# The first layer's gate columns in three chunks of 512 and its last value columns in two of 384, with the fill beside the attention set from 64 to 48

## The reference

```
proj = h @ w_in
na_qkv, na_gate, dn_qkv, dn_gate, dn_ba, mem_q, mem_gate = split_cols(
    proj, [3 * NA_W, NA_W, 3 * DN_W, DN_W, 4 * DN_HEADS, MEM_W, MEM_W])
...
na_o = merge_heads(neighbourhood_attention(q, k, v, na_rpb)) * jax.nn.silu(na_gate)
dn_o = deltanet_branch(dn_qkv, dn_ba, ...) * jax.nn.silu(dn_gate)
mem_o = memory_branch(mem_q, mem_n, w_mem_kv, ...) * jax.nn.silu(mem_gate)
return x + jnp.concatenate([na_o, dn_o, mem_o], axis=-1) @ w_out
```

## Time and profile before

| what | value |
|---|---|
| median of 3 runs | 3140.31 us (3139.92 to 3143.08) |
| time of the profiled execution | 3142.65 us |
| its span, first to last instruction | 3140.9 us |
| mean granted TensorE clock | 0.990 |
| PE, DVE, ACT busy | 97%, 58%, 48% of the span |
| the attention of the first layer | from 554.4 to 662.0 us of the span |

### The profile page before, as it was taken

One profiled execution on the slowest core, in us unless ns is written; L12 is line 12 of the kernel. 1 busy time (PEld: TensorE's weight loads), 2 busy tenths in 40 slices (PEclk: granted clock), 3 DMA queues, 4 the chain that ended last, 5 costly groups with the idle time before them and its releaser, 6 DMA issues.

```text
span 3140.9 us, 36907 instructions
## 1 busy us (share of the span) xinstructions
PE 3049.4 (97%) x15084; PEld 2588.2 (82%) x15084; DVE 1810.5 (58%) x2348; ACT 1517.4 (48%) x2332; POOL 9.4 (0%) x10
## 2 busy tenths in 40 slices
PE   6999999999999999999999999999999999999999
PEld 5878888878877788989888888888889888888887
DVE  4686666555555455665666545555575675554554
ACT  4654333554555555544546444444554545444443
POOL 0000000000000000000000000000000000000000
PEclk8999999999999999999999999999999999999999
DMA  6553222456544556544544656656544544555654
GB/s 230 163 174 108 94 68 94 135 181 227 176 160 148 172 174 209 183 147 147 174 161 161 203 196 204 207 185 209 190 155 139 175 161 163 188 199 189 218 190 155
DMA packets 273433, 534.92 MB, mean 170 GB/s; under 512 B 8912, under 2 KB 50000, under 8 KB 271216
## 3 DMA queue, kind: packets, MB, share of 16 engines
q1 hardware_dynamic: 268976, 509.12, 49.3%
q10 hardware_dynamic: 4288, 23.44, 1.9%
HBM read 523.09 MB, written 9.44 MB: 170 GB/s over the span
## 4 chain that ended last, share of the span: by engine, by line
PE 85%; DVE 7%; ACT 5%; DVEq 2%; issue 1%; ACTq 0%; DMA 0%; SPq 0%
PE acc L377 25%; PE acc L379 25%; PE acc L378 25%; DVE w_lo L340 2%; PE tb L671 1%; ACT w_hi L330 1%; PE tb L875 1%; PE tb L2230 1%; PE tb L882 1%; PE tb L881 1%; PE tb L2105 1%; DVE stat L2058 0%; PE tb L2103 0%; DVE sq L2056 0%; PE tb L1132 0%
## 5 line engine op out<-in xcount | busy, mean ns | idle before, releaser
L340 DVE TENSOR_TENSOR w_lo<-raw,w_hi 128x1024 fp32r<-128x1024 f32 (+3 forms) x1008 | 1140.4, 1170 | 678.6 <-ACT w_hi L330 668.6
L330 ACT ACTIVATE w_hi<-raw 128x1024 fp32r<-128x1024 f32 (+3 forms) x1008 | 986.3, 1016 | 570.2 <-PE acc L379 548.1
L377 PE MATMUL acc<-w_hi,x_hi 128*128 128x512 f32 (+4 forms) x2880 | 1126.7, 391 | 29.9 <-DVE w_lo L340 29.8
L379 PE MATMUL acc<-w_hi,x_lo 128*128 128x512 f32 (+4 forms) x2880 | 1092.3, 379 | 0.0
L378 PE MATMUL acc<-w_lo,x_hi 128*128 128x512 f32 (+4 forms) x2880 | 1090.8, 379 | 0.0
L377 PEld LDWEIGHTS acc<-w_hi,x_hi 128*128 128x128 f32 x2880 | 547.1, 190 | 124.3 <-DVE w_lo L340 32.2
L379 PEld LDWEIGHTS acc<-w_hi,x_lo 128*128 128x128 f32 x2880 | 546.0, 190 | 93.9
L378 PEld LDWEIGHTS acc<-w_lo,x_hi 128*128 128x128 f32 x2880 | 547.5, 190 | 84.6
L377 PE MATMUL acc<-w_hi,mB_hi 128*128 128x512 f32 x256 | 100.6, 393 | 0.0
L379 PE MATMUL acc<-w_hi,mB_lo 128*128 128x512 f32 x256 | 99.8, 390 | 0.0
L378 PE MATMUL acc<-w_lo,mB_hi 128*128 128x512 f32 x256 | 99.7, 389 | 0.0
(11 more groups left out here) (483 smaller groups left out, 3473.1 us busy)
## 6 DMA issues: line engine op xcount, KB each, us to landing
raw<-in_h_w_in SPq DMA_DIRECT2D x184, 1024.0 KB, 4.9
raw<-in_o_w_in SPq DMA_DIRECT2D x56, 1024.0 KB, 5.0
raw<-in_e_w_in SPq DMA_DIRECT2D x48, 1024.0 KB, 5.0
raw<-in_h_w_branch SPq DMA_DIRECT2D x48, 1024.0 KB, 5.0
raw<-in_h_w_out SPq DMA_DIRECT2D x32, 1024.0 KB, 4.9
raw<-in_h_w_in SPq DMA_DIRECT2D x40, 768.0 KB, 4.3
raw<-in_e_w_out SPq DMA_DIRECT2D x16, 1024.0 KB, 5.0
raw<-in_o_w_out SPq DMA_DIRECT2D x16, 1024.0 KB, 5.0
```

Source lines behind the costliest of these rows:

```text
L330: act.activation(k.w_hi[:, a % HI_SLOTS, rows, :width], k.raw[:, a % SLOTS, rows, :width], ACT.Copy).then_inc(k.hi_ready, 1)
L340: e.tensor_tensor(k.w_lo[:, a % SLOTS, rows, :width], k.raw[:, a % SLOTS, rows, :width], k.w_hi[:, a % HI_SLOTS, rows, :width].bitcast(F32 ...
L377: pe.matmul(out, x_hi[:, tok], wh, start=first, stop=False)
L379: mm = pe.matmul(out, x_lo[:, tok], wh, start=False, stop=last)
```

## The change

The columns of the weight matrix are laid out on the host so that the DN gate and the NA gate stand next to each other (1536 columns), and are projected in three chunks of 512; the middle one is copied out in parts, two blocks to `dgate` and two to `ngate`. The last 768 columns of NA q, k, v become two chunks of 384 in place of one of 512 and one of 256. The gates' steps fall from 64 to 48, and `ATT_FILL` with them, so that the same eight steps, now 512 wide, stay for after the attention. The two silus on ACT move from after visit 26 to after visit 33, and DVE's multiplications from after visit 30 to after visit 36. (All lines of the changed file stand two lower from here on: L1151 is L1153 there.)

```diff
+DN_COL, GATE_COL, MEM_COL = 2304, 4632, 6168
...
-DN_FILL, ATT_FILL = 104, 64
+DN_FILL, ATT_FILL = 104, 48
...
-    c["N"] = add(k, w, 0, 4, x, into(k.na, 0), **a)
-    c["N"] += add(k, w, 2048, 1, x, into(k.na, 16, 2), width=256, **a)
-    c["MQ"] = add(k, w, BA_COL + BA, 1, x, into(k.mq4, 0), **a)
-    c["MG"] = add(k, w, BA_COL + BA + 512, 1, x, into(k.mg, 0), **a)
-    c["DG"] = add(k, w, 5376 + BA, 1, x, into(k.dgate, 0), **a)
-    c["DG"] += add(k, w, 5376 + BA + 512, 1, x, into(k.dgate, 4, 2), width=256, **a)
-    c["NG"] = add(k, w, 2304, 1, x, into(k.ngate, 0), **a)
-    c["NG"] += add(k, w, 2304 + 512, 1, x, into(k.ngate, 4, 2), width=256, **a)
+    c["N"] = add(k, w, 0, 3, x, into(k.na, 0), **a)
+    c["N"] += add(k, w, 1536, 2, x, into(k.na, 12, 3), width=384, **a)
+    c["MQ"] = add(k, w, MEM_COL, 1, x, into(k.mq4, 0), **a)
+    c["MG"] = add(k, w, MEM_COL + 512, 1, x, into(k.mg, 0), **a)
+    g = add(k, w, GATE_COL, 1, x, into(k.dgate, 0), **a)
+    g += add(k, w, GATE_COL + 512, 1, x, lambda i: lambda t: (k.dgate[:, 4:6, t, :], k.ngate[:, 0:2, t, :]), "parts", **a)
+    g += add(k, w, GATE_COL + 1024, 1, x, into(k.ngate, 2), **a)
+    c["DG"], c["NG"] = g[:2], g[1:]
...
-        if i == 26:
+        if i == 33:
             act_silu(k, act, PART_DN, k.named["DG"])
             act_silu(k, act, PART_MEM, k.named["MG"])
...
-        elif i == 30:
+        elif i == 36:
             dve.drain()
             dve_gated(k, dve, PART_DN, 1)
             dve_gated(k, dve, PART_MEM, 2)
...
-    return np.concatenate([w[:, :5376], w[:, BA_COL:BA_COL + BA], w[:, 5376:BA_COL], w[:, BA_COL + BA:]], axis=1)
+    na, nag, dn, dng, ba, mem = np.split(w, [2304, 3072, 5376, 6144, 6144 + BA], axis=1)
+    return np.concatenate([na, dn, ba, dng, nag, mem], axis=1)
```

More of the change, by code:

```diff
@@ L35 @@
 BA = 4 * DN_H
-BA_COL = 6144
+DN_COL, GATE_COL, MEM_COL = 2304, 4632, 6168
 O_Q, O_K, O_V, O_G = (0, 12, 24), (4, 16, 28), (8, 20, 32), (44, 48, 52)
@@ L504, in plan_even @@
     a = dict(by="act", rstd=2)
-    c["D"] = add(k, w, 3072, 4, x, into(k.dn_p, 0), need=lambda kt: kt // 2 + 1, **a)
-    c["D"] += add(k, w, 3072 + 2048, 1, x, lambda i: lambda t: (k.dn_p[:, 16:18, t, :], k.ba_cols[:, t, :]), "parts",
+    c["D"] = add(k, w, DN_COL, 4, x, into(k.dn_p, 0), need=lambda kt: kt // 2 + 1, **a)
+    c["D"] += add(k, w, DN_COL + 2048, 1, x, lambda i: lambda t: (k.dn_p[:, 16:18, t, :], k.ba_cols[:, t, :]), "parts",
                   width=256 + BA, **a)
```

## The result

The changed kernel takes 3147.53 us in the median of 15 runs (3144.85 to 3152.03), the kernel before on the same chips 3141.53 (3139.37 to 3143.69). The ratio is 1.0022, with a 95% interval of 1.0014 to 1.0030 (the ratio is taken over all runs; the two medians alone give 1.0019): slower by 6 us. That is clear of the interval, and close to the 0.2% that the prediction set as the limit of what can be told from no change. The profiled execution took 3147.54 us, its span is 3145.7, against 3142.65 and 3140.9 before.

A forecast was written before the change was run, and what follows sets the result against it. PE's issue time and waits bound the kernel (PE busy 97%). Matmuls -1.0, attention waits with low clock +5.1, deltanet -0.4 sum to +3.7 us: 3144.0 us from a median of 3140.31, range 3138 to 3149 (the forecast's own 3142 to 3146.3).

The forecast's parts named there:

- The matmuls: PE, deltanet steps 48 to 79: 192 matmuls of 384 columns replace 288 of 256, saving 1.0 us.
- The last pair: Attention, unit 8: PE waits 6.5 us for the exponential behind copies, silus and a quad's split.
- The fourth pair: Attention, units 6 and 7: the split of visit 27 between two exponentials makes PE wait 2.7 us.
- Elsewhere: Attention: waits of 1.4 us in the second pair, 0.7 in the third, none found in the first.
- The low clock: Attention: half clock costs 1.6 us after the wait of 6.5 and 0.8 after that of 2.7.
- The attention's sum: First fill to last product: about 106.5 us, with steps and visits 92.8 and waits 13.7.
- The eight steps behind: Fill left after the attention: 11.0 us in place of 5.7, so 5.3 more, no gain of their own.
- The deltanet: Second half of the deltanet stage: cover gained and lost gives -0.4 us, bounds -1.4 and +2.
- The rival by which only the silus' wait comes: Attention: the small waits don't come, only 6.5 + 1.6; -1.9 us, 3138.4; chance 0.20.
- the one by which nothing happens but 96 matmuls fewer: Whole kernel: waits as before, -1.0 us, 3139.3; chance 0.08.
- The slow rival: Low clock after both waits, deltanet waits (+2.4), late last splits from DVE's multiplications (+2): +8.9, 3149.2; chance 0.16.
- The fast rival: Attention: cover on every visit absorbs every chain, the silus too; -10 us, 3130; chance 0.06.

The follow-up runs named there:

- e1: The changed kernel with ACT's silus after visit 37 in place of 33 and DVE's multiplications after 39 in place of 36: 3143.02 us, ratio 1.0002.
- f3: The changed kernel with fill steps in another phase (24 added before the division by 40) from visit 33 on only: 3137.87 us, ratio 0.9994.
- f4: The changed kernel with fill steps in another phase (24 added before the division by 40) for visits 16 to 31 only: 3142.34 us, ratio 1.0003.
- f1: The changed kernel with fill steps in another phase (24 added before the division by 40) from visit 16 on: 3136.42 us, ratio 0.9983.
- e2: The kernel before with only the last 768 columns of NA q, k, v in two chunks of 384: 3140.84 us, ratio 0.9995.
- e3_gates_only: The changed kernel with NA q, k, v back in four chunks of 512 and one of 256: 3149.36 us, ratio 1.0023.

## Why the prediction was right, point by point

- *The matmuls (-1.0).* The count and the price of a matmul hold: 96 fewer, and unbroken 384-wide steps in the changed kernel are about 0.175 us apart (446.06 to 446.94 has five). It can't be seen apart from the rest in the time.
- *The last pair (wait 6.5).* 5.89, at the place, in the order and by the chain given; the copies of the chunk in four parts follow each other in 0.36 us, not 0.42. e1 and f3 show the cause: with the silus out of the way it is 0.7, with the split ahead of them and a step more of cover 1.4. The comparison that the prediction made beside it was too high: unit 7's exponential cost 0.88 us before the change (at 631.92), not "some 1.5"; the sum doesn't use it.
- *The fourth pair (2.7).* 2.25; f4 shows the cause.
- *Elsewhere (1.4 and 0.7).* 0.79 and 0.28. Waits in all 11.3 forecast, 9.2 shown.
- *The low clock (1.6 + 0.8).* This was too small: 4.6 us at half speed after the long wait, which cost about 2.3 us, and 3.4 us after the wait of 2.25 (0.66 over 5 us), about 1.7, where I had put 0.8. Together 4.0 in place of 2.4.
- *The attention's sum.* 106.5 us forecast, 106.8 measured, and the closeness is partly luck: waits 2.1 too high, low clock 1.6 too low, and 0.8 us in neither. The work priced at 92.8 took 93.3 us in f1, whose attention has no low clock (95.5 less waits of 2.2).
- *The eight steps behind (+5.3).* +5.7; a wait of 0.24 for `yB_lo` grew to 0.69.
- *The deltanet (-0.4).* The step that was mis-sized in sign: +0.2 in the traces, and e2 can't tell it from nothing. The cover lost in steps 48 to 63 opened waits of 0.41, 0.74 and 1.08 us (at 409.62, 422.55 and 425.24), which I had put into the bound alone.

The sum by places is +5.0 against +3.7 forecast. The medians differ by 6.0; the remaining 1 us isn't explained, and lies inside the interval (4.4 to 9.4 us). Stretches in which the program is the same differ by 2 us between the two profiled executions, so a sum from one trace of each can't be closed to 1 us. The changed kernel's 3147.53 us lies 1.2 above the forecast's own range (3142 to 3146.3) and inside the whole one; the kernel before, beside it, was itself 1.2 above the median that the forecast started from.

The rival by which only the silus' wait comes is refuted: all four waits came. So is the one by which nothing happens but 96 matmuls fewer. The slow rival (+8.9) was half right, and the measured +6.0 lies midway between it and the forecast (+3.7): both waits were followed by low clock, as it said; the deltanet gave 0.6 us more than my value, not 2.4; and DVE's multiplications after visit 36 held up nothing that PE waited for. They took 2.9 us (649.49 to 652.38), not the 4.6 of the kernel before, and no wait of PE for a split stands between 650 and 690 us. The fast rival, in which even cover absorbs every chain, failed on its condition, program order; with the order mended (f1) the same 48 steps come near it in the attention, which is 11.2 us shorter than the changed kernel's and 12.1 shorter than before, where cover on every visit would give 14.8 (107.6 to 92.8). Of this 5.7 us come back behind the attention, and the time is 4.8 us under the kernel before, about half of the 10 that it named.

## What to carry to other kernels

Where engines work through hand-written programs and fill is dealt out by a formula, a change of its amount moves the turns of everything that hangs on its count (here: the split of a quad every fourth step). Look for the visit in which such a turn falls between two links of a latency chain, above all beside a long block like a table load; dealing the steps out in another phase in one pair took 4 and 8 us out of the attention here (in the second case about 1.7 of it because a low clock in another pair stayed away), more than the 1 us that the change of the work itself was worth. Count a long wait of PE together with the low clock behind it, and try the phase before giving up on less fill.

## What the runs showed of the hardware

A wait of PE of about 2 us was followed by low clock in some executions and not in others. In the changed kernel, after the wait of 2.25 us at 625.30, the window above shows 0.66 over 5 us. The kernel f3_last_pair has the same program up to visit 31 and the same wait at 623.61, and e3_gates_only has the same wait at 624.84. In both the clock stays high:

```profile
623.60:628.60 5.00, 4.99 (x33) 1.00 0.74 274
...
624.80:629.80 5.00, 4.96 (x32) 1.00 0.77 283
```

e3's attention is 1.9 us shorter for it (104.8 against 106.8) with the same four waits. The wait of 2.1 us in the deltanet shows the same: in the changed kernel, at 496.58, and in f3, at 496.47, with the same instructions ahead of it:

```profile
496.58:501.58 5.00, 5.00 (x24) 0.66 0.00 0
...
496.47:501.47 5.00, 5.00 (x37) 1.00 0.00 0
```

Of the ten profiles eight have low clock there, and f1 and f3 don't. e1's wait of 2.80 us at 655.20 was followed by none (1.00 over 5 us), and the wait of 3.26 us before the change by 0.55 over 3.2 us. The wait of 5.89 us was followed by low clock in each of the three profiles that had it, for 4.6 us in the changed kernel, about 4.1 in e3 and 5.8 in f4 (granted 0.50), which cost about half of that, 2.0 to 2.9 us.

The Trainium skill (TensorE: Matmul & The Clock Gate, "What's actually happening") holds that the point of transition varies with the phase of a free-running monitor. The pairs of traces above, in which the program and the wait are alike and the clock isn't, fit with that; no run here shows the phase itself.
